# Feed-forward inputs split before their norm's reciprocal root is known, the root multiplied in at evacuation

## What is computed

```python
def rms_norm(x, w):
    y = xf * lax.rsqrt(jnp.mean(xf * xf, axis=-1, keepdims=True) + NORM_EPS)
    return (y * w.astype(jnp.float32)).astype(x.dtype)

def swiglu_ffn(x, w_gate, w_up, w_down):
    return (jax.nn.silu(x @ w_gate) * (x @ w_up)) @ w_down

for l in range(DEPTH):          # DEPTH = 2
    ...
        x = x + merged @ w_out[l]
        x = x + swiglu_ffn(rms_norm(x, ffn_norm[l]), w_gate[l], w_up[l], w_down[l])
```

## Time and profile before

| | |
|---|---|
| median of 3 runs | 2307.31 us |
| the runs | 2307.64, 2302.64, 2307.31 us |
| profiled execution, its own time | 2303.84 us |
| its span, first to last instruction | 2302.1 us |
| mean granted TensorE clock | 0.959 |
| TensorE busy | 2120.3 us (92%) |
| VectorE busy | 1144.4 us (50%) |
| ScalarE busy | 758.9 us (33%) |
| GpSimd busy | 538.6 us (23%) |
| weights DMA, 296 issues of 512 KB | 3.5 us each to landing |

### The profile page before, as it was taken

The page is one execution under the profiler, slowest core; times in us unless marked ns, Lnnn a source line. Parts: engine busy times, 40 slices in busy tenths (PEclk is TensorE's granted clock), DMA queues, the critical chain, the costliest instruction groups (busy, mean ns, idle before and its releaser), DMA issues.

```text
span 2302.1 us, 25818 instructions
## 1 busy us (share of the span) xinstructions
PE 2120.3 (92%) x10100; PEld 1676.2 (73%) x10100; DVE 1144.4 (50%) x1575; ACT 758.9 (33%) x1149; POOL 538.6 (23%) x300
## 2 busy tenths in 40 slices
PE   5989998899999899999988889888999998999998
PEld 3667976667677688888756679766566776888886
DVE  6344569763347544432273365796533475444321
ACT  5333231264334322222152332313642343222221
POOL 2336027523116000000032350374131250000000
PEclk9999999999989999999989999999989899999999
DMA  4232011222124223333233310123121342332332
GB/s 144 101 104 80 15 46 60 83 69 69 55 102 166 80 92 100 94 100 101 67 99 101 117 49 15 51 69 97 55 69 42 126 153 69 100 101 92 101 101 92
DMA packets 55124, 197.03 MB, mean 86 GB/s; under 512 B 6112, under 2 KB 6112, under 8 KB 52576
## 3 DMA queue, kind: packets, MB, share of 16 engines
q1 hardware_dynamic: 43488, 161.85, 22.1%
q10 hardware_dynamic: 11520, 33.56, 3.8%
HBM read 176.51 MB, written 18.87 MB: 85 GB/s over the span
## 4 chain that ended last, share of the span: by engine, by line
PE 36%; DVE 8%; POOL 2%; ACT 2%; DMA 1%; issue 1%; SPq 0%; POOLq 0%; DVEq 0%; PEldq 0%; ACTq 0%
PE bank L455 9%; PE bank L457 9%; PE bank L456 9%; DVE arena L1636 2%; DVE arena L1631 1%; DMA raw<-weights 1%; PE bank L904 1%; PE bank L662 1%; PE bank L865 1%; PE bank L642 1%; POOL wL L1859 1%; PE bank L792 1%; DVE wL L1320 1%; DVE arena L1802 1%; ACT wH L1005 0%
## 5 line engine op out<-in xcount | busy, mean ns | idle before, releaser
L455 PE MATMUL bank<-hH,wH 128*128 128x512 f32 (+1 forms) x1536 | 620.7, 404 | 54.9 <-POOL wL L1859 27.4
L456 PE MATMUL bank<-hL,wH 128*128 128x512 f32 (+1 forms) x1536 | 609.9, 397 | 0.0
L457 PE MATMUL bank<-hH,wL 128*128 128x512 f32 (+1 forms) x1536 | 608.4, 396 | 0.0
L1859 POOL TENSOR_TENSOR wL<-raw,wH 128x1024 fp32r<-128x1024 f32 x114 | 281.6, 2474 | 1232.7 <-ACT wH L1005 1232.5
L1005 ACT ACTIVATE wH<-raw 128x1024 fp32r<-128x1024 f32 x276 | 290.2, 1053 | 395.9 <-PE bank L457 231.7
L455 PEld LDWEIGHTS bank<-hH,wH 128*128 128x128 f32 (+1 forms) x1536 | 294.9, 192 | 135.3 <-issue 36.4
L457 PEld LDWEIGHTS bank<-hH,wL 128*128 128x128 f32 (+1 forms) x1536 | 293.6, 191 | 65.6 <-issue 1.0
L456 PEld LDWEIGHTS bank<-hL,wH 128*128 128x128 f32 (+1 forms) x1536 | 294.4, 192 | 61.8 <-issue 1.0
L1320 DVE TENSOR_TENSOR wL<-raw,wH 128x1024 fp32r<-128x1024 f32 x162 | 213.3, 1317 | 185.3 <-ACT wH L1005 185.2
L1008 ACT ACTIVATE gst<-bank 128x512 f32<-128x512 f32 x64 | 38.2, 596 | 351.1 <-PE bank L457 351.1
L457 PE MATMUL bank<-hidH,wL 128*128 128x512 f32 x352 | 140.4, 399 | 0.0
(11 more groups left out here) (380 smaller groups left out, 3008.1 us busy)
## 6 DMA issues: line engine op xcount, KB each, us to landing
raw<-weights SPq DMA_DIRECT2D x296, 512.0 KB, 3.5
gates<-gst ACTq DMA_DIRECT2D x64, 256.0 KB, 2.4
gload<-gates ACTq DMA_DIRECT2D x16, 1024.0 KB, 6.9
xT<-x SPq DMA_DIRECT2D x1, 2048.0 KB, 10.1
out<-xT SPq DMA_DIRECT2D x1, 2048.0 KB, 6.7
const<-constants SPq DMA_DIRECT2D x1, 1228.5 KB, 5.5
pack<-params SPq DMA_DIRECT2D x2, 451.0 KB, 3.9
cosT<-pos SPq DMA_DIRECT2D x1, 256.0 KB, 5.6
```

The costliest lines, as they stand in the source:

```text
L455: mm(out, a[0], b[0], start=start, stop=False)
L456: mm(out, a[0], b[1], start=False, stop=False)
L457: return mm(out, a[1], b[0], start=False, stop=stop)
L1859: tt_(wL[:, ORD[i] % SPLIT], raw[:, i % RING], wH[:, ORD[i] % SPLIT].bitcast(F32), SU)\
```

## The change

The input of the feed-forward products is no longer the normed x but x times the norm weight. It doesn't depend on the reciprocal root, so hH[k] and hL[k] are made in the output stage, tile by tile: ScalarE copies xT[k] scaled by the weight to hH[k] just ahead of the square, VectorE makes hL[k] as xT[k] times weight minus hH[k] (`ffn_input`) one output tile later. The squares are added up in sequence on VectorE instead of in pairs, so one ones product remains; it stands behind fg0 and fu0. ScalarE then makes the root, after it has split slab fu1.

The root is multiplied in when the products are evacuated: VectorE multiplies the gate product by rs2 into fa (`ga_ready`, counted twice per f now), ScalarE takes tanh from fa, VectorE forms (tanh + 1) * fa, then multiplies the up product by rs2 into fb, and fa times fb halved gives fh. After these the steps are as before. Bank numbers shift by two, and rs2 and fb lie in crot, a buffer of the mixing block.

```diff
--- before.py
+++ after.py
@@ -403,8 +403,10 @@
         PTN = [sum(m // 2 + 1 for m in range(k)) for k in range(2 * NT + 1)]
         mtmp = arena[:, 8192:12288].rearrange("p (a m s) -> p a m s", a=2, m=4)
         hs2 = arena[:, 8192:12288].rearrange("p (k s) -> p k s", k=KT)
-        rs2 = arena[:, 0:512]
         ft, fa, fh = comp[:, 0:2, :], comp[:, 2:4, :], tiles(11264, 2)
+        crot_flat = crot[:, :, :, :].rearrange("p r c s -> p (r c s)")
+        rs2 = crot_flat[:, 0:512]
+        fb = crot_flat[:, 512:1536].rearrange("p (a s) -> p a s", a=2)
 
         with nc.Fori(0, DEPTH) as layer:
             with nc.Block() as block:
@@ -932,29 +934,28 @@
                             last = mm3(b[:, :], parts(w, ALLP, k), parts((mH, mLow), ALLP, k), k == 0, k == KT - 1)
                         last.then_inc(q["slab_done"], 1)
 
-                    for k in range(1, KT, 2):
-                        pe.wait_ge(q["sq_pair"], KT // 2 + k // 2 + 1)
-                        last = mm(PS[2][:, :], ones, hs2[:, k, :], start=(k == 1), stop=(k == KT - 1))
-                    last.then_inc(q["ss_ps"], 1)
-
                     w = [slab("fg0"), slab("fu0")]
                     for k in range(KT):
                         pe.wait_ge(q["h_ready"], KT + k + 1)
                         for j in range(2):
-                            last = mm3(PS[j][:, :], parts(w[j], ALLP, k), parts(h2p, ALLP, k), k == 0, k == KT - 1)
+                            last = mm3(PS[2 + j][:, :], parts(w[j], ALLP, k), parts(h2p, ALLP, k), k == 0, k == KT - 1)
                             if k == KT - 1:
                                 last.then_inc(q["slab_done"], 1)
+                    pe.wait_ge(q["sq_pair"], KT // 2 + 1)
+                    mm(PS[0][:, :], ones, hs2[:, KT - 1, :], start=True, stop=True).then_inc(q["ss_ps"], 1)
                     for f in range(1, FT):
                         for j, name in enumerate(("fg", "fu")):
                             w = slab(f"{name}{f}")
-                            b = PS[2 * (f % 4) + j]
+                            b = PS[2 * ((f + 1) % 4) + j]
+                            if f == 3:
+                                pe.wait_ge(q["rstd_ready"], 2)
                             if f >= 4:
                                 pe.wait_ge(q["hid_tmp"], f - 3)
                             for k in range(KT):
                                 last = mm3(b[:, :], parts(w, ALLP, k), parts(h2p, ALLP, k), k == 0, k == KT - 1)
                             last.then_inc(q["slab_done"], 1)
                     for dt in range(KT):
-                        b = PS[4 + dt % 4]
+                        b = PS[(6 + dt % 4) % 8]
                         if dt >= 4:
                             pe.wait_ge(q["dn_taken"], dt - 3)
                         elif dt == 0:
@@ -1281,17 +1282,14 @@
                     for k in range(KT):
                         high_to(ahead(SLAB[f"out{k}"]))
                         a.wait_ge(q["xo_ready"], k + 1)
+                        act(hH[:, k, :], xT[:, k, :], ACT.Copy, scale=prm("fn")[:, k:k + 1]).then_inc(q["h_high"], 1)
                         act(hs2[:, k, :], xT[:, k, :], ACT.Square).then_inc(q["sq_ready"], 1)
+                    high_to(ahead(SLAB["fg0"]))
                     a.wait_ge(q["ss_ps"], 2)
-                    rsqrt(rs2, PS[2][:, :], D, q["rstd_ready"])
-                    for k in range(KT):
-                        a.wait_ge(q["h_tmp"], KT + k + 1)
-                        act(hH[:, k, :], hs2[:, k, :], ACT.Copy).then_inc(q["h_high"], 1)
+                    rsqrt(rs2, PS[0][:, :], D, q["rstd_ready"])
                     for f in range(FT):
-                        a.wait_ge(q["slab_done"], SLAB[f"fg{f}"] + 1)
-                        if f >= 2:
-                            a.wait_ge(q["ga_ready"], f - 1)
-                        act(ft[:, f % 2, :], PS[2 * (f % 4)][:, :], ACT.Tanh, scale=0.5).then_inc(q["fg_tanh"], 1)
+                        a.wait_ge(q["ga_ready"], 2 * f + 1)
+                        act(ft[:, f % 2, :], fa[:, f % 2, :], ACT.Tanh, scale=0.5).then_inc(q["fg_tanh"], 1)
                         high_to(ahead(SLAB[f"fg{f}"]))
                         a.wait_ge(q["hid_tmp"], f + 1)
                         act(hidH[:, f, :], fh[:, f % 2, :], ACT.Copy).then_inc(q["hid_high"], 1)
@@ -1805,35 +1803,41 @@
                             merged_low(dt - 1)
                         low_to(ahead(SLAB[f"br{dt}"]))
                     merged_low(KT - 1)
+                    def ffn_input(k):
+                        v.wait_ge(q["h_high"], KT + k + 1)
+                        stt(hL[:, k, :], xT[:, k, :], prm("fn")[:, k:k + 1], hH[:, k, :].bitcast(F32), M, SU)\
+                            .then_inc(q["h_ready"], 1)
+
                     def add_squares(k):
                         v.wait_ge(q["sq_ready"], KT + k + 1)
-                        tt_(hs2[:, k, :], hs2[:, k, :], hs2[:, k - 1, :], A_).then_inc(q["sq_pair"], 1)
+                        return tt_(hs2[:, k, :], hs2[:, k, :], hs2[:, k - 1, :], A_)
 
                     for dt in range(KT):
                         v.wait_ge(q["slab_done"], SLAB[f"out{dt}"] + 1)
                         stt(xT[:, dt, :], PS[dt % 2][:, :], 0.5, xT[:, dt, :], M, A_).then_inc(q["xo_ready"], 1)
                         low_to(ahead(SLAB[f"out{dt}"]))
-                        if dt % 2 and dt > 1:
-                            add_squares(dt - 2)
-                    add_squares(KT - 1)
-
-                    v.wait_ge(q["rstd_ready"], 2)
-                    for k in range(KT + 1):
-                        if k < KT:
-                            stt(hs2[:, k, :], xT[:, k, :], prm("fn")[:, k:k + 1], rs2, M, M).then_inc(q["h_tmp"], 1)
-                        if k:
-                            v.wait_ge(q["h_high"], KT + k)
-                            low(hL[:, k - 1, :], hs2[:, k - 1, :], hH[:, k - 1, :]).then_inc(q["h_ready"], 1)
+                        if dt:
+                            ffn_input(dt - 1)
+                        if dt > 1:
+                            step(add_squares(dt - 1))
+                    ffn_input(KT - 1)
+                    add_squares(KT - 1).then_inc(q["sq_pair"], 1)
+                    low_to(ahead(SLAB["fg0"]))
 
                     for f in range(FT):
+                        v.wait_ge(q["slab_done"], SLAB[f"fg{f}"] + 1)
+                        if f == 0:
+                            v.wait_ge(q["rstd_ready"], 2)
+                        tt_(fa[:, f % 2, :], PS[2 * ((f + 1) % 4)][:, :], rs2, M).then_inc(q["ga_ready"], 1)
+                        low_to(ahead(SLAB[f"fg{f}"]))
                         v.wait_ge(q["fg_tanh"], f + 1)
-                        stt(fa[:, f % 2, :], ft[:, f % 2, :], 1.0, PS[2 * (f % 4)][:, :], A_, M).then_inc(q["ga_ready"], 1)
-                        low_to(ahead(SLAB[f"fg{f}"]))
-                        v.wait_ge(q["ga_ready"], f + 1)
+                        stt(fa[:, f % 2, :], ft[:, f % 2, :], 1.0, fa[:, f % 2, :], A_, M)
+                        v.wait_ge(q["slab_done"], SLAB[f"fu{f}"] + 1)
+                        tt_(fb[:, f % 2, :], PS[2 * ((f + 1) % 4) + 1][:, :], rs2, M).then_inc(q["ga_ready"], 1)
+                        v.wait_ge(q["ga_ready"], 2 * f + 2)
                         if f >= 2:
                             v.wait_ge(q["hid_ready"], f - 1)
-                        v.wait_ge(q["slab_done"], SLAB[f"fu{f}"] + 1)
-                        stt(fh[:, f % 2, :], fa[:, f % 2, :], 0.5, PS[2 * (f % 4) + 1][:, :], M, M).then_inc(q["hid_tmp"], 1)
+                        stt(fh[:, f % 2, :], fa[:, f % 2, :], 0.5, fb[:, f % 2, :], M, M).then_inc(q["hid_tmp"], 1)
                         v.wait_ge(q["hid_high"], f + 1)
                         low(hidL[:, f, :], fh[:, f % 2, :], hidH[:, f, :]).then_inc(q["hid_ready"], 1)
                         low_to(ahead(SLAB[f"fu{f}"]))
@@ -1841,7 +1845,7 @@
                         for j in range(3):
                             low_to(ahead(SLAB[f"dn{dt}_{j}"]))
                         v.wait_ge(q["slab_done"], SLAB[f"dn{dt}_2"] + 1)
-                        tt_(xT[:, dt, :], xT[:, dt, :], PS[4 + dt % 4][:, :], A_).then_inc(q["dn_taken"], 1)
+                        tt_(xT[:, dt, :], xT[:, dt, :], PS[(6 + dt % 4) % 8][:, :], A_).then_inc(q["dn_taken"], 1)
 
                 @block.gpsimd
                 def _(g):
```

## The result

| | before | changed |
|---|---|---|
| median | 2307.47 us (4 runs) | 2281.41 us (4 runs) |
| lowest to highest | 2302.64 to 2311.08 | 2278.56 to 2284.44 |
| profiled execution, own time / span | 2303.84 / 2302.1 us | 2280.53 / 2278.7 us |
| mean granted TensorE clock | 0.959 | 0.958 |
| VectorE busy | 1144.4 us | 1197.5 us |

The ratio of changed to before is 0.9891, 95% interval 0.9876 to 0.9905. The forecast was 2283 us.

What follows compares the result with a forecast made beforehand. TensorE was taken as the bound, busy 2120.3 of 2302.1 us, with idling and slow products at the feed-forward norm. 2302.1 - 22.9 = 2279.2 us of span, 2280.9 or 2284.4 by run group, so 2283; range 2277 to 2291.

Steps and rivals of the forecast that it cites:

- The stretch: Last output product to fg1's first: 48 products at clock 1.00 and one ones product, 11.8 us instead of 22.71 and 23.79.
- The gains of 10.9 and 12.0 us: Shortening of the way from output products to fg1 in the first and second layer, 22.9 us in both.
- the 10.1 us ahead of the products: Time between output and feed-forward products in each layer before the change, described as 10 us of mostly idling.
- Inputs in time: Output stage's end: hL[6] ready at +3.4 and hL[7] at +4.9 us, needed at +8.2 and +9.5; four microseconds of cover each.
- the 0.15 allowed: ScalarE's scaled copy to hH[k]: 0.64 us, with 0.0 to 0.15 more allowed for the scale read per partition.
- The root: Ln and Exp with two table loads behind fu1's split; fg2 ready at 793.35, wanted at 794.3, slack 0.9 us.
- Rival (a): Late root makes TensorE wait in both layers, 2 to 5 us in all, about 2287; chance 0.13.
- The round: Steady feed-forward loop: serial VectorE and ScalarE steps sum to 8.6 us against TensorE's 10.88, slack 2.3, cost nothing.
- VectorE waits for TensorE twice in each round: Sign in the feed-forward loop: from f = 1 on VectorE waits for TensorE once or twice in each round.
- a round of 11.4 us on: Feed-forward round length from which the change is slower than before, 2.8 us above the predicted sum; that rival's chance 0.03.
- Rival (b): Half-clock stretches fall elsewhere behind the first norm: +-3 us, 2280 to 2286; chance 0.81 together with the forecast.
- two groups of executions of the kernel before: Runs at 2302.64 and 2303.84, and at 2307.31 and 2307.64; same gain expected in either, giving 2280.9 or 2284.4.

Runs made afterwards that it cites:

- e1: Kernel before the change, plus six unread filler products per layer in TensorE's idle time at the feed-forward norm; ratio to the kernel before 0.9963.
- e3: Changed kernel with squares added in pairs again and four ones products instead of one, behind fg0 and fu0; 2287.60 us, ratio to the kernel before 0.9927.
- e5: Changed kernel with four more 128 x 512 copies on ScalarE between the root's Exp and its ready signal; 2287.12 us, one execution.
- e6: Changed kernel with three more VectorE operations in each feed-forward round, ahead of the gate product's evacuation; 2286.20 us, one execution.
- e7: Changed kernel with six more VectorE operations in each feed-forward round, ahead of the gate product's evacuation; 2361.69 us, one execution.
- e2: Changed kernel with the ones product and its wait for the squares put ahead of fg0 and fu0 again; 2298.05 us, ratio to the kernel before 0.9974.
- e9: Changed kernel with three filler products per layer behind the sum of squares at the layer-start norm; 2281.82 us, ratio to the kernel before 0.9916.
- e4: Changed kernel with twelve fillers per layer at the layer-start norm, seven ahead of the sum of squares, five behind; 2291.2 us, ratio to the kernel before 0.9938.
- e8: Changed kernel with VectorE making the odd squares at the layer-start norm, one filler ahead of the sum and four behind; 2284.86 us, ratio to the kernel before 0.9923.

## Why the prediction was right

**The stretch.** Forecast 11.8 us from the last output product to fg1 (11.8 to 12.1), measured 10.91 + 0.86 = 11.8. This is the mechanism that was forecast, not only its size. The gains of 10.9 and 12.0 us were met to 0.1 in both layers, since all their terms were durations that the trace of before showed at other places: 48 products at clock 1.00, a ones product, and two starts in TensorE's timeline. e1 and e3 confirm the division into gap, clock and ones products. One thing the prediction says loosely: the 10.1 us ahead of the products were 6.2 of idling and 3.9 of ones products.

**Inputs in time.** Forecast hL[6] at +3.4 and hL[7] at +4.9 us, demanded at +8.2 and +9.5. VectorE's and ScalarE's timelines of the changed kernel, first layer, with the end of the output products at 775.20:

```profile
777.70 0.75 DVE L1808 SCALAR_TENSOR_TENSOR hL<-xT,pack,hH 128x512 fp32r<-128x512 f32 x1
...
779.08 0.75 DVE L1808 SCALAR_TENSOR_TENSOR hL<-xT,pack,hH 128x512 fp32r<-128x512 f32 x1
779.75 0.68 DVE L1813 TENSOR_TENSOR arena<-arena 128x512 f32<-128x512 f32 x1
...
790.71 0.69 DVE L1831 TENSOR_TENSOR comp<-bank,crot 128x512 f32<-128x512 f32 x1 [2.70 <-ACT crot L1043]
...
795.77 1.23 DVE L1318 TENSOR_TENSOR wL<-raw,wH 128x1024 fp32r<-128x1024 f32 x1 [0.26 <-ACT wH L1006]
```

```profile
776.43 0.71 ACT L1285 ACTIVATE hH<-xT,pack 128x512 fp32r<-128x512 f32 x1
...
786.77 1.28 ACT L1042 ACT_TABLE_LOAD   x1
...
788.68 1.28 ACT L1043 ACT_TABLE_LOAD   x1
789.98 0.63 ACT L1043 ACTIVATE crot<-crot 128x512 f32<-128x512 f32 x1
```

hL[6] (L1808) ends at 778.45, +3.3, and hL[7] at 779.83, +4.6. The scaled copy (L1285) takes 0.71 us rather than 0.64, inside the 0.15 allowed.

**The root.** Table load, Ln, table load, Exp run as the rows of before have them: the second load ends at 789.96 and Exp starts at 789.98. Rival (a) stayed out. The Trainium skill (ScalarE: Activation LUTs, What ACT_TABLE_LOAD costs) adds some 1.38 us of draining to a load; the trace of the changed kernel doesn't agree with that either: 0.02 us lie between Ln's end (788.06 + 0.60) and the load, and 0.02 between the load and Exp. The low part of fg2 ends at 795.77 + 1.23 = 797.00 and TensorE takes it up at 797.86: slack 0.86, forecast 0.9. e5 used it up and got the wait, of 1.67 us in each layer.

**The round.** Forecast 8.6 us of serial steps. Measured in rounds that don't wait: 8.28. The small difference is mostly that VectorE, where it doesn't wait, starts an operation some 0.08 us before the record of the one ahead ends (the low part of 795.77 lasts until 797.00, the next evacuation starts at 796.91), at three places in the round; the sum left that out. In the steady loop VectorE waits for TensorE twice in each round, as foreseen:

```profile
814.38 0.69 DVE L1831 TENSOR_TENSOR comp<-bank,crot 128x512 f32<-128x512 f32 x1 [0.83 <-PE bank L459]
...
819.82 0.69 DVE L1836 TENSOR_TENSOR crot<-bank,crot 128x512 f32<-128x512 f32 x1 [1.27 <-PE bank L459]
```

The forecast had the change come out slower from a round of 11.4 us on. e6 (10.46) and e7 (12.63, slower than the kernel before) lie on either side of it.

**What was mis-sized, and luck.** Rival (b) put the moving of half-clock stretches at +-3 us. It is more. The stretch from the first projection product to the first branch product, the same code in every kernel here, took between 650.1 and 657.6 us. Busy time by stretch, the kernel before in both layers, and e3 in the second:

```profile
27.61:677.71 650.10, 589.45 (x3067) 459.74 (x3067) 360.71 (x546) 223.89 (x392) 224.78 (x122) 0.95 0.20 66
1166.66:1824.26 657.60, 597.40 (x3067) 464.74 (x3067) 358.74 (x546) 223.83 (x392) 224.47 (x122) 0.94 0.20 65
```

```profile
1160.67:1810.93 650.26, 595.85 (x3067) 465.39 (x3067) 358.61 (x546) 223.84 (x392) 223.49 (x122) 0.94 0.20 66
```

Over 22 such stretches of eleven executions, the granted clock is 0.93 to 0.95 and the TensorE busy time 589 to 601 us for the same products. The length varies by up to 7.5 us per layer. It doesn't go with the busy time alone (650.10 us at 589.45, and 650.26 at 595.85), so how much of it is the clock is not shown. In the profiles compared it came out as +3.5 and -5.8, nearly zero in the sum. The medians give 26 us on one chip and 21 on another for a gain of 22.9; both intervals (21.9 to 28.6, and 17.3 to 29.2) hold 22.9, so a spread of this size is enough for that difference. The forecast of 2283 was put between two groups of executions of the kernel before; 23 later executions of it lie between 2299.5 and 2312.1 without such groups, so that the median came within 2 us of 2283 owes something to luck, while the 22.9 us do not. What decides when the clock falls within these stretches stays open.

## What to carry to other kernels

A per-token scale can be taken out of the input of a product and put into its evacuation, so that the product no longer waits for a reduction over all of the input. Its worth is what TensorE idles for, plus the slow products behind, plus what the reduction on TensorE can be shortened by (e3: 5.2 us of the 22.9), and it is only had in full if every step that the reduction still needs of TensorE stands behind other work (e2: 16 of the 22.9 us hang on this). Before adding to evacuation, sum up the serial round of the engines that also prepare the weights; as long as it is shorter than TensorE's part, additions are free in the steady rounds (the first round, with less slack, cost 1.7 us per layer in e6), and beyond that each microsecond counts once per round (e7).

## What the runs showed of the hardware

- TensorE's clock fell to its lower level within an idle time of 5.1 us (e2, granted clock 0.50 from 779.00, with work resumed at 780.44). In the kernel before it was low behind 10.1 us with 3.9 us of ones products in them (0.86 and 0.79 over the next 48 products). In e7 it stayed up over waits of 1.45 us, but behind the waits of 3.37 us it was 0.50 for some 3.4 us. In e9 it was 0.50 behind a wait of only 2.3 us, shortly after a longer low stretch.
- Fillers held the clock where they started at full clock in the 10.1 us gap (e1: TensorE busy for 9.0 of the 10.1, clock 1.00 behind it). They did harm where it was already low (e4: 9.1 us for seven, of which 6 us at clock 0.50), and three of them ahead of a wait of 2.3 us did not hold it (e9).
- VectorE operations with two SBUF inputs of 128 x 512 took 2.7 to 2.8 us beside GpSimd's slab work and 0.68 to 0.69 otherwise (e8).
